# Attention's keys transposed and split between the steps of the SSM forward, its small inputs loaded there too

## The reference, cut to what matters

```python
p = rms_norm(x) @ w_in
q, k, v, z, xbc, dt_raw, mq = split(p)
q, k = rope(rms_norm(q), pos), rope(rms_norm(k), pos)
attn_out = windowed_gqa(q, k, v, attn_sink)      # 16 query heads, 4 key heads, |i - j| <= 128, a sink logit per head
ssm_out  = ssd_bidirectional(z, xbc, dt_raw)     # chunks of 128 tokens, backward scan and forward scan, gate, RMS norm
mem_out  = memory_attention(mq, mk, mv)          # 256 memory tokens
x = x + concat(attn_out, ssm_out, mem_out) @ w_out
x = x + w_down(silu(g) * u),  [g, u] = dwconv(rms_norm(x) @ w_ffn_up)
```

## Time and profile before

| what | us |
|---|---|
| three runs, median (lowest to highest) | 2209.69 (2207.54 to 2212.36) |
| the profiled execution's own time | 2212.37 |
| its span | 2210.6 |
| stretch 550 to 690 of the span (the SSM forward) | 140 |
| stretch 690 to 717.5 (attention up to its first score) | 27.5 |
| stretch 717.5 to 937 (the rest of attention) | 219.5 |

### The profile page before, as it was taken

How to read it: one execution, slowest core, us unless ns; L and a number is a source line. 1 busy time by engine, 2 the same in 40 slices (tenths; PEclk the granted TensorE clock), 3 DMA queues, 4 the chain that set the end, 5 groups by cost and what they waited for, 6 DMA issues and landing times. The chain is left out here.

```text
span 2210.6 us, 30145 instructions
## 1 busy us (share of the span) xinstructions
PE 2035.6 (92%) x10642; PEld 1735.0 (78%) x10642; DVE 1365.7 (62%) x1936; ACT 608.4 (28%) x1172; POOL 232.3 (11%) x242
## 2 busy tenths in 40 slices
PE   4999999996774999886999889999999999999997
PEld 3887888884674999875788778888888888888885
DVE  6664686235773888754423546766766766766766
ACT  5111121110673666641102321121121121121120
POOL 2000584040342100000000000000000000000000
PEclk7999999998776999988999999999999999999998
DMA  5323223213543111134511031010010010121002
GB/s 172 108 83 119 86 100 105 81 43 116 197 163 128 39 49 39 43 108 145 210 43 43 21 106 30 29 57 29 28 57 29 28 56 29 28 56 29 28 9 95
DMA packets 111118, 164.05 MB, mean 74 GB/s; under 512 B 8736, under 2 KB 68160, under 8 KB 109760
## 3 DMA queue, kind: packets, MB, share of 16 engines
q1 hardware_dynamic: 81648, 118.98, 16.8%
q10 hardware_dynamic: 29392, 44.07, 5.7%
HBM read 125.45 MB, written 37.57 MB: 74 GB/s over the span
## 5 line engine op out<-in xcount | busy, mean ns | idle before, releaser
L2398 PE MATMUL ff_proj<-h_hi,ff_uhi 128*128 128x512 f32 (+1 forms) x1056 | 374.5, 355 | 11.0 <-DVE ff_ulo L2311 11.0
L2398 PE MATMUL ff_proj<-h_lo,ff_uhi 128*128 128x512 f32 (+1 forms) x1056 | 374.3, 354 | 0.0
L2398 PE MATMUL ff_proj<-h_hi,ff_ulo 128*128 128x512 f32 (+1 forms) x1056 | 373.9, 354 | 0.0
L2357 DVE TENSOR_TENSOR x<-x,ff_proj 128x512 f32<-128x512 f32 x264 | 181.6, 688 | 185.3 <-PE ff_proj L2418 183.0
L2398 PEld LDWEIGHTS ff_proj<-h_hi,ff_uhi 128*128 128x128 f32 x1056 | 200.0, 189 | 40.1 <-DVE ff_ulo L2311 11.4
L2398 PEld LDWEIGHTS ff_proj<-h_lo,ff_uhi 128*128 128x128 f32 x1056 | 200.1, 189 | 28.6
L2398 PEld LDWEIGHTS ff_proj<-h_hi,ff_ulo 128*128 128x128 f32 x1056 | 199.9, 189 | 27.9
L576 PE MATMUL pj_bank<-pj_whi,act_hi 128*128 128x512 f32 x400 | 155.7, 389 | 0.0
L576 PE MATMUL pj_bank<-pj_whi,act_lo 128*128 128x512 f32 x400 | 155.6, 389 | 0.0
L576 PE MATMUL pj_bank<-pj_wlo,act_hi 128*128 128x512 f32 x400 | 155.6, 389 | 0.0
L2269 ACT ACTIVATE ff_padded<-ff_proj 128x1024 f32<-128x1024 f32 x44 | 45.3, 1028 | 350.4 <-PE ff_proj L2398 350.4
(11 more groups left out here) (267 smaller groups left out, 4219.9 us busy)
## 6 DMA issues: line engine op xcount, KB each, us to landing
ff_rawu<-w_up SPq DMA_DIRECT2D x44, 512.0 KB, 4.9
pj_raw<-w_in SPq DMA_DIRECT2D x28, 512.0 KB, 3.7
ff_rawd<-w_down SPq DMA_DIRECT2D x22, 512.0 KB, 3.5
sf_rows<-scratch_acs_rows SPq DMA_DIRECT2D x10, 1024.0 KB, 7.6
wo_raw<-w_out SPq DMA_DIRECT2D x16, 512.0 KB, 4.3
scratch_proj<-hd_pieces ACTq DMA_DIRECT2D x30, 256.0 KB, 2.1
n_x<-tokens SPq DMA_DIRECT2D x14, 512.0 KB, 4.3
wo_mix<-scratch_mix ACTq DMA_DIRECT2D x9, 640.0 KB, 3.9
```

What stands on the lines that cost most here:

```text
L2357: nc.vector.tensor_tensor(v, v, ring(g), ALU.add).then_inc(added, 1)
L2398: m = nc.tensor.matmul(proj[:, g, t0:t0 + n], U[w][:, s, k, g], X[x][:, k, t0:t0 + n], start=(k == 0 and r == 0), stop=(k == KC - 1 and r ...
```

## The change

The identity, the mask, the sink, the values, the split keys and the two query slots become buffers that live from before the SSM to the end (`AttentionInputs`). Attention loads none of them any more and makes no keys; its lists begin with the split of the first query tile. The SSM forward makes the keys, one tile in each step:

- SP loads the keys of tile t behind z into one of two slots; after the last step it loads the sink, the mask, the values and the first two query tiles, and waits for them.
- TensorE makes the four transposes into one new PSUM buffer, `k_ps`, between `turn` and y_off. Except in the first step it waits there until VectorE has subtracted the keys of t-1.
- ScalarE copies the high part at the end of its body, VectorE subtracts at the end of its own, behind the norm.

```diff
 def attention(nc, proj, ahead, mix_t):
         def _(sp):
-            keys(0)
-            sp.dma_start(ident[:, :], ident_dram).then_inc(S["const"], 16)
-            sp.dma_start(q_raw[:, 0], proj[0:P, 0:1024]).then_inc(q_loaded[0], 16)
-            keys(1)
-            keys(2)
-            sp.dma_start(sinkb[:, :], sink.broadcast_to([P, HQ])).then_inc(S["const"], 16)
-            sp.dma_start(mask[:, :], mask_dram[1]).then_inc(S["mask"], 16)
-            sp.dma_start(v_sb[:, :, :], kv[:, :, 1280:1536]).then_inc(S["vl"], 16)
...
         def _(act):
             high(act, 0, 0)
-            for t in range(NT):
-                act.wait_ge(S["kt"], t + 1)
-                nc.scalar.activation(kt_hi[:, :, t * P:(t + 1) * P], key_bank(t), ACT.Copy
-                                     ).then_inc(S["khi"], 1)
...
         def _(dve):
-            for t in range(NT):
-                dve.wait_ge(S["khi"], t + 1)
-                v.tensor_tensor(kt_lo[:, :, cols], key_bank(t), kt_hi[:, :, cols].bitcast(FP32),
-                                ALU.subtract).then_inc(S["klo"], 1)
...
         def _(pe):
-            for t in range(NT):
-                pe.wait_ge(k_loaded[sum(t >= t0 for t0, _ in KEY_PARTS[1:])], 16)
-                if t >= 4:
-                    pe.wait_ge(S["klo"], t - 3)
-                for j in range(HKV):
-                    m = T.transpose(key_bank(t)[:, j], k_two[:, t, j], ident[:, :])
-                m.then_inc(S["kt"], 1)
-            pe.wait_ge(S["klo"], NT)
...
 def ssm_forward(nc, proj, xbc_c, acs_rows, ident_dram, small, R, mix_t, ahead, k_twice, mask_dram):
+        k_two = b.sb("sf_ktwo", [P, 2, HKV, 2 * DH])
+        k_ps = b.ps("sf_kps", [P, HKV, P])
         def _(sp):
                 sp.dma_start(z[:, s], proj[r, 1536:2048]).then_inc(z_loaded[s], 16)
+                if not before(t, 2):
+                    sp.wait_ge(S["kt"], t - 1)
+                keys = k_twice[r].rearrange("p (h d) -> p h d", h=HKV)
+                sp.dma_start(k_two[:, s], keys).then_inc(k_loaded[s], 16)
             order(sp, load)
+            for dst, src in (sink, mask, v, q tile 0, q tile 1):
+                sp.dma_start(dst, src).then_inc(ahead_loaded, 16)
+            sp.wait_ge(ahead_loaded, 16 * 5)
         def _(pe):   # body(t, s)
                     m = T.transpose(m_ps[:, g], xc[:, s, (4 + g) * P:(5 + g) * P], ident[:, :])
                 m.then_inc(S["turn"], 1)
+                pe.wait_ge(k_loaded[s], loaded_value(t, s))
+                if not first:
+                    pe.wait_ge(S["klo"], t)
+                for h in range(HKV):
+                    m = T.transpose(k_ps[:, h], k_two[:, s, h], ident[:, :])
+                m.then_inc(S["kt"], 1)
         def _(act):  # body(t, s)
                 if not before(t, 2):
                     store(t - 2, before(t, 3))
+                act.wait_ge(S["kt"], t + 1)
+                a.activation(ahead.kt_hi[:, :, cols(t)], k_ps[:, :, :], ACT.Copy).then_inc(S["khi"], 1)
         def _(dve):  # body(t, s)
                 if not before(t, 1):
                     norm(t - 1, 1 - s, before(t, 3))
+                dve.wait_ge(S["khi"], t + 1)
+                v.tensor_tensor(ahead.kt_lo[:, :, cols(t)], k_ps[:, :, :], ahead.kt_hi[:, :, cols(t)].bitcast(FP32),
+                                ALU.subtract).then_inc(S["klo"], 1)
```

More of the change, by code:

```diff
@@ L767, in _, with __init__, attention @@
             act.wait_ge(row_stored, 32 * NCH)
-def attention(nc, proj, k_twice, ident_dram, mask_dram, small, mix_t):
-    sink = small["attn_sink"]
+class AttentionInputs:
+    def __init__(self, nc, ctx):
+        b = Bufs(nc, ctx)
+        self.ident = b.sb("at_ident", [P, P])
+        self.mask = b.sb("at_mask", [P, 3 * P])
+        self.sinkb = b.sb("at_sink", [P, HQ])
+        self.v_sb = b.sb("at_v", [P, NT, HKV * DH])
+        self.kt_hi = b.sb("at_kthi", [P, HKV, TOK], F32R)
+        self.kt_lo = b.sb("at_ktlo", [P, HKV, TOK], F32R)
+        self.q_raw = b.sb("at_qraw", [P, 2, HQ, DH])
+def attention(nc, proj, ahead, mix_t):
     WIN = 3 * P
-    KEY_PARTS = ((0, 2), (2, 4), (6, NT - 6))
     with ExitStack() as ctx:
         b = Bufs(nc, ctx)
[L785 to L791, removed]
+        ident, mask, sinkb, v_sb = ahead.ident, ahead.mask, ahead.sinkb, ahead.v_sb
+        kt_hi, kt_lo, q_raw = ahead.kt_hi, ahead.kt_lo, ahead.q_raw
         nsink = b.sb("at_nsink", [P, HQ])
-        q_raw = b.sb("at_qraw", [P, 2, HQ, DH])
         q_two = b.sb("at_qtwo", [P, HQ, 2, DH])
@@ L807, in attention @@
         x_ps = b.ps("at_xps", [P, 2, 4, P])
-        names = ("const", "vl", "kt", "khi", "klo", "table", "qhi", "qlo", "s", "m", "e", "t", "pt", "v",
-                 "den", "oscaled", "x", "xcopy", "mask", "ready")
+        names = ("table", "qhi", "qlo", "s", "m", "e", "t", "pt", "v",
+                 "den", "oscaled", "x", "xcopy", "ready")
         S = {n: b.sem(f"at_s_{n}") for n in names}
-        q_loaded, k_loaded = b.sems("at_ql", 2), b.sems("at_kl", len(KEY_PARTS))
+        q_loaded = b.sems("at_ql", 2)
         stored = b.sem("at_stored")
@@ L818, in window @@
             return int(first), 3 - int(last)
-        def key_bank(t):
-            return t_ps[:, t % 4] if t % 4 < 2 else s_ps[:, t % 4 - 2].rearrange("p (h n) -> p h n", n=P)
         def tile_loop(engine, body):
@@ L836, in _ @@
         def _(sp):
[L837 to L843, removed]
-            keys(0)
-            sp.dma_start(ident[:, :], ident_dram).then_inc(S["const"], 16)
-            sp.dma_start(q_raw[:, 0], proj[0:P, 0:1024]).then_inc(q_loaded[0], 16)
-            keys(1)
-            keys(2)
-            sp.dma_start(sinkb[:, :], sink.broadcast_to([P, HQ])).then_inc(S["const"], 16)
-            sp.dma_start(mask[:, :], mask_dram[1]).then_inc(S["mask"], 16)
-            sp.dma_start(v_sb[:, :, :], kv[:, :, 1280:1536]).then_inc(S["vl"], 16)
             def load(t, s):
-                if not (isinstance(t, int) and t < 2):
-                    sp.wait_ge(S["qlo"], t - 1)
-                if isinstance(t, int) and t == 0:
+                if isinstance(t, int) and t < 2:
                     return
+                sp.wait_ge(S["qlo"], t - 1)
                 rows = slice(t * P, (t + 1) * P) if isinstance(t, int) else ds(t * P, P)
@@ L878, in q_loaded_value @@
         def q_loaded_value(t, s):
-            return 16 * (t // 2 + 1) if isinstance(t, int) else 8 * (t - s) + 16
+            return 16 * (t // 2) if isinstance(t, int) else 8 * (t - s)
         def units_before(t):
@@ L892, in high @@
         def high(act, t, s):
-            act.wait_ge(q_loaded[s], q_loaded_value(t, s))
+            if not (isinstance(t, int) and t < 2):
+                act.wait_ge(q_loaded[s], q_loaded_value(t, s))
             if not (isinstance(t, int) and t == 0):
@@ L951, in _ @@
             v = nc.vector
-            dve.wait_ge(S["const"], 16 * 2)
             v.tensor_scalar(nsink[:, :], sinkb[:, :], -1.0, None, ALU.mult).then_inc(S["table"], 1)
             v.tensor_scalar(sm[:, :, 0], sinkb[:, :], -1.0, None, ALU.mult).then_inc(S["table"], 1)
-            for t in range(NT):
-                cols = slice(t * P, (t + 1) * P)
-                dve.wait_ge(S["khi"], t + 1)
-                v.tensor_tensor(kt_lo[:, :, cols], key_bank(t), kt_hi[:, :, cols].bitcast(FP32),
-                                ALU.subtract).then_inc(S["klo"], 1)
             def finish(t, s, c):
@@ L1005, in _ @@
             dve.wait_ge(S["table"], 2)
-            dve.wait_ge(S["mask"], 16)
             tile_loop(dve, tile)
@@ L1014, in _ @@
             T = nc.tensor
-            pe.wait_ge(S["const"], 16 * 2)
-            for t in range(NT):
-                pe.wait_ge(k_loaded[sum(t >= t0 for t0, _ in KEY_PARTS[1:])], 16)
-                if t >= 4:
-                    pe.wait_ge(S["klo"], t - 3)
-                for j in range(HKV):
-                    m = T.transpose(key_bank(t)[:, j], k_two[:, t, j], ident[:, :])
-                m.then_inc(S["kt"], 1)
-            pe.wait_ge(S["klo"], NT)
             def q_unit(c, n):
@@ L1032, in q_unit @@
                 m.then_inc(S["x"], 1)
-            pe.wait_ge(S["vl"], 16)
             pe.wait_ge(S["qlo"], 1)
@@ L1515, in _, with ssm_forward @@
             order(dve, body, reset)
-def ssm_forward(nc, proj, xbc_c, acs_rows, ident_dram, small, R, mix_t):
+def ssm_forward(nc, proj, xbc_c, acs_rows, ident_dram, small, R, mix_t, ahead, k_twice, mask_dram):
     XW = NS * PS
@@ L1526, in ssm_forward @@
         b = Bufs(nc, ctx)
-        ident = b.sb("sf_ident", [P, P])
+        ident = ahead.ident
+        k_two = b.sb("sf_ktwo", [P, 2, HKV, 2 * DH])
         wn = b.sb("sf_wn", [P, XW])
@@ L1558, in ssm_forward @@
         t_ps = b.ps("sf_tps", [P, 4, P])
+        k_ps = b.ps("sf_kps", [P, HKV, P])
+        k_loaded, ahead_loaded = b.sems("sf_kl", 2), b.sem("sf_ahead")
         S = {n: b.sem(f"sf_s_{n}") for n in (
+            "kt", "khi", "klo",
```

(22 more changed lines are left out.)

## The result

The changed kernel takes 2218.33 us at the median of six runs (2213.86 to 2225.62), the kernel before 2210.02 (six runs): ratio 1.004, 95% interval 1.0028 to 1.0052. It is slower, by 8.3 us; 14.6 were forecast.

A forecast was written before the change was run, and what follows sets the result against it. The forward was taken as bound by a chain of hand-offs, attention's head by one serial path. Forward 5.0 + 25.5 + 1.6 = 32.1 us more, attention 17.5 less: +14.6 on 2209.7, forecast 2224 us, range 2208 to 2238.

The forecast's parts named there:

- The mechanism: Forward: key transposes wait for VectorE's last subtract, so y_off, CB and W (32 matmuls of L1629) queue behind the norm.
- a sign of being wrong: Any of: key transposes waiting for a DMA, y_off before the norm, W's lengths shifting one way, attention's head above 12 us.
- The head: Attention's start to first score: 17.5 us saved, ends 16 and 19.7, with 1.6 us lost to POOL's semaphore clears.
- The first step: Forward's start to the first W: 5.0 us longer, ends 4.1 and 6.2; the first key tile holds y_off some 2 us.
- The clock, "which I cost at no change": TensorE's clock in the forward: alternation between fast and slow steps costed as unchanged despite a new wait in every step.
- the seven steps: W 0 to 6 and 8 to the next: 3.65 us more each, 25.5 in all, ends 20.3 and 30.5.
- the slow price of 30.5: Upper end for the seven steps: keys, y_off and CB at the slow clock, 4.35 us more a step.
- the reset step: Forward, W 6 to W 7, where the state is reset: subtract and four slow transposes add 1.6 us, ends 1.0 and 2.0.
- Rival 2: Forward: every W falls to the slow clock, four fast ones adding 13.5 us; +33, total 2243 us; chance 0.13.
- Rival 1: Forward: wait before CB is short, only VectorE's 0.69 us added per step; -6, total 2204 us; chance 0.09.
- rival 3: Forward: the key tile's DMA, issued behind z, lands late; +10 us on top, total 2234 us; chance 0.05.
- Rival 4: Forward grows only 13 to 22 us as W to norm shortens, VectorE's products waiting for nobody; 2210 us; chance 0.07.

The follow-up runs named there:

- Late keys: Changed kernel with the four key transposes moved behind the state's matmuls of the same step; 2199.9 us, ratio 0.9946 to the kernel before.
- the wait alone: Key transposes moved behind the state's matmuls, but TensorE still waits for the last subtract ahead of y_off; 2211.75 us, ratio 1.0009 to the kernel before.
- the run with five semaphores fewer: Changed kernel with keys loaded, transposed and split in attention as before, only the other inputs loaded in the forward; 2200.95 us, ratio 0.9954 to the kernel before.
- second profile: Changed kernel run once more, unaltered, for a second profiled execution; 2217.03 us, ratio 1.0034 to the kernel before.
- the filled changed kernel: Changed kernel with 36 idle transposes of the identity ahead of the key transposes in each step; 2206.62 us, ratio 0.9976 to the kernel before.

## Why the prediction was right, and where its size was off

**The mechanism** was right: the wait for the last subtract ahead of y_off, with CB and W queued behind. Late keys against the wait alone shows it. Key transposes right behind the subtract, y_off behind the norm, W 4.6 to 4.9 us behind it, steps of 13.7 to 15.8 us: as it said. The forward took 160.8 us (552.26 to 713.08), not 172, and one thing that it had named as a sign of being wrong did come: W's lengths shifted in one direction.

**The head** was right to 0.1 us in the profile, POOL's late start included (1.64, 1.6 estimated); its reason, the clears, is borne out by the run with five semaphores fewer. That the loads beside the keys carry half of it was not said.

**The first step** was right: +5.4 for +5.0, and the first key tile held TensorE 2.26 us.

**The clock, "which I cost at no change"**, is the step that failed. The part of the sum that was worked out, from the norm to W, came out somewhat larger: over the seven steps +29.0 us for 25.5, close to the slow price of 30.5, as keys and y_off are slow in every step and not in every second one. The part that was set at nothing, from W to the next norm, came out 10.3 us shorter, 8.4 of it W itself (27.0 us instead of 35.4). In the reset step W is 3.25 us shorter, at the end 1.64. So W's fast clock alone gave back 13.3 us; the table's sum (+3.2) falls 11.4 short of 14.6.

The Trainium skill (TensorE: Matmul & The Clock Gate, HAM oscillation) says that a group of matmuls which comes after such a wait starts at the slow clock; the trace agrees for the keys (1.06 to 1.11 us in nine of ten steps, against 0.63 where the gap was filled). Rival 2 carried that on to W. W here stands behind 3.15 us of other work: of the seven with such a path (W 1 to 6 and 8) five took 3.68 us and two 3.86 and 3.88, with one of 6.93 in the second profile.

**Rival 1** (the wait short) and **rival 3** (the tile late) did not happen here; the late tile came at once when the bank was doubled, as it lands 2.9 us after an issue that stands behind z. **Rival 4** was nearer than its 0.07: its size for the forward (13 to 22 us) holds the 20.6 measured, and from W to the norm the time did get shorter, but mostly by W's clock and not by VectorE's products.

## What to carry to other kernels

Work moved into another loop's gaps has to be placed behind what the loop's chain waits for, in the order of its engine's list: the same instructions cost 18 us between two places. Before giving an engine a second buffer, look at which wait is next. Where TensorE waits in short gaps on a chain that it closes itself, price that chain at both clocks, and try what idle transposes in the gap bring (8 and 10 a step paid here; 36 paid too, but not in the step where they stood on the path).

## What the hardware showed that I had not expected

With a longer wait, the costliest work behind it was faster: with TensorE idle 4.9 us the keys and y_off ran at 1.2 GHz and W behind them, in nearly every step, at 2.4, where with gaps of 1 to 2 us W itself alternated between 3.7 and 6 to 7 us. Why it alternates there is not shown beyond this: with the gaps filled it no longer does, but for one W of 5.60. 18 idle transposes a step, 2.3 us of TensorE's time (1.04 and 1.26), shortened late keys by 10 us. Two kernels spread differently, and the reason is not shown: 12 runs of the wait alone lie within 16 us, 10 of the filled changed kernel within 4.
